# Unit-matrix products that nothing reads, put ahead of some forty waits of TensorE in a two-stage transformer kernel

## What is computed

```python
def first_block(x, c, ctx, c_ctx, w_mod, ...):          # two layers, streams x and z = ctx, 256 x 1024 each
    for l in range(DEPTH):
        mx = jnp.split((jax.nn.silu(c) @ w_mod[l] + b_mod[l])[:, None, :], N_MOD, axis=-1)
        mz = jnp.split(jax.nn.silu(c_ctx) @ w_mod[l] + b_mod[l], N_MOD, axis=-1)
        x = x + 0.5 * mx[2] * swiglu(modulate(rms_norm(x), mx[0], mx[1]), ffn1_w1[l], ffn1_w3[l], ffn1_w2[l])
        z = z + 0.5 * mz[2] * swiglu(modulate(rms_norm(z), mz[0], mz[1]), ffn1_w1[l], ffn1_w3[l], ffn1_w2[l])
        hx = modulate(rms_norm(x), mx[3], mx[4]) @ w_in[l]
        hz = modulate(rms_norm(z), mz[3], mz[4]) @ w_in[l]
        mix_x, mix_z = token_mixing(hx, hz, ...)         # Fourier, neighborhood, gated linear, grouped-query heads
        x = x + mx[5] * (mix_x @ w_out[l])
        x = x + 0.5 * mx[8] * swiglu(modulate(rms_norm(x), mx[6], mx[7]), ffn2_w1[l], ffn2_w3[l], ffn2_w2[l])
        if not last:                                     # the same two lines for z
...
def second_block(x, mem, positions, w_in, b_gate, ...):
    for l in range(DEPTH):
        h = x @ w_in[l]
        c_q, c_kv, k_pe, dq, dk, dv, mq, gate_pre = jnp.split(h, splits, axis=-1)
        o_mla = _mla_branch(...)                         # latent attention, 8 heads
        o_diff = _diff_branch(...)                       # differential attention, 8 heads x 2 maps
        o_mem = _mem_branch(mq, mem, mem_w_kv[l])        # attention to 256 rows of memory
        g = jax.nn.sigmoid(gate_pre.reshape(b, s, N_BRANCH, d) + b_gate[l])
        merged = g[:, :, 0] * (o_mla @ ...) + g[:, :, 1] * (o_diff @ ...) + g[:, :, 2] * (o_mem @ ...)
        x = _layernorm(DEEPNORM_ALPHA * x + merged @ w_out[l], ln1_g[l], ln1_b[l])
        f = jnp.square(jax.nn.relu(x @ mlp_w1[l])) @ mlp_w2[l]
        x = _layernorm(DEEPNORM_ALPHA * x + f, ln2_g[l], ln2_b[l])
    return x
```

## Time and profile before

| | |
|---|---|
| three runs | 3268.85, 3278.03, 3303.54 us; median 3278.03 |
| profiled execution | 3283.36 us; span from the first to the last instruction 3281.5 us |
| mean granted TensorE clock | 0.963 |
| busy: PE, DVE, ACT, POOL | 3116.6, 1765.1, 1506.8, 146.6 us |
| transfers | 552 MB read from memory, 169 GB/s |

### The profile page before, as it was taken

The page is one execution under the profiler, slowest core; times in us unless marked ns, Lnnn a source line. Parts: engine busy times, 40 slices in busy tenths (PEclk is TensorE's granted clock), DMA queues, the critical chain, the costliest instruction groups (busy, mean ns, idle before and its releaser), DMA issues.

```text
span 3281.5 us, 53932 instructions
## 1 busy us (share of the span) xinstructions
PE 3116.6 (95%) x22930; PEld 2821.6 (86%) x22930; DVE 1765.1 (54%) x2769; ACT 1506.8 (46%) x2294; POOL 146.6 (4%) x143
## 2 busy tenths in 40 slices
PE   7999999998999999999999899999998999999898
PEld 5899788897779998899898778999898898989887
DVE  3446544554436545446555434555666557576655
ACT  3345445453444443345444334446654444665443
POOL 0000100000000000000100000000110101101000
PEclk9999989998999999999999779999999999999999
DMA  7765435653535555765355335555345564434553
GB/s 260 263 206 168 155 117 169 229 185 116 155 121 191 179 181 191 253 218 169 129 171 169 103 105 191 180 168 155 121 150 186 168 204 151 142 113 153 178 191 131
DMA packets 465132, 556.66 MB, mean 170 GB/s; under 512 B 25421, under 2 KB 431869, under 8 KB 464509
## 3 DMA queue, kind: packets, MB, share of 16 engines
q1 hardware_dynamic: 464892, 553.21, 52.5%
HBM read 552.12 MB, written 1.05 MB: 169 GB/s over the span
## 4 chain that ended last, share of the span: by engine, by line
PE 81%; DVE 9%; DMA 3%; ACT 3%; issue 2%; SPq 1%; POOL 0%; DVEq 0%; ACTq 0%
PE psum L121 23%; PE psum L123 22%; PE psum L122 22%; DVE wl L2137 2%; DMA wr<-in_ffn_w_dram 2%; DVE wl L272 1%; PE psum L692 1%; PE psum L1492 1%; PE psum L2292 1%; PE psum L2398 1%; PE psum L2376 1%; PE psum L1848 1%; PE psum L1941 1%; PE psum L1479 1%; PE psum L1167 1%
## 5 line engine op out<-in xcount | busy, mean ns | idle before, releaser
L272 DVE TENSOR_TENSOR wl<-wr,wh 128x1024 fp32r<-128x1024 f32 (+1 forms) x558 | 656.8, 1212 | 241.8 <-ACT wh L261 240.5
L261 ACT ACTIVATE wh<-wr 128x1024 fp32r<-128x1024 f32 (+1 forms) x558 | 555.6, 1039 | 173.2 <-DMA wr<-in_ffn_w_dram 154.1
L121 PE MATMUL psum<-xt_hi,wh 128*128 128x256 f32 (+1 forms) x2000 | 574.2, 287 | 7.8 <-DVE wl L2137 4.8
L122 PE MATMUL psum<-xt_lo,wh 128*128 128x256 f32 (+1 forms) x2000 | 563.3, 282 | 0.0
L123 PE MATMUL psum<-xt_hi,wl 128*128 128x256 f32 (+1 forms) x2000 | 563.3, 282 | 0.0
L2137 DVE TENSOR_TENSOR wl<-wr,wh 128x1024 fp32r<-128x1024 f32 (+3 forms) x336 | 389.7, 1200 | 78.9 <-ACT wh L2129 77.6
L121 PEld LDWEIGHTS psum<-xt_hi,wh 128*128 128x128 f32 (+1 forms) x2000 | 380.1, 190 | 20.5 <-DVE wl L2137 8.3
L122 PEld LDWEIGHTS psum<-xt_lo,wh 128*128 128x128 f32 (+1 forms) x2000 | 379.7, 190 | 2.0
L123 PEld LDWEIGHTS psum<-xt_hi,wl 128*128 128x128 f32 (+1 forms) x2000 | 380.3, 190 | 0.1
L121 PE MATMUL psum<-wh,xt_hi 128*128 128x256 f32 (+1 forms) x1280 | 369.2, 288 | 4.3 <-DVE wl L272 2.4
L2129 ACT ACTIVATE wh<-wr 128x1024 fp32r<-128x1024 f32 (+3 forms) x336 | 322.6, 997 | 104.2 <-DMA wr<-in_mlp_w_dram 75.3
(11 more groups left out here) (489 smaller groups left out, 5505.4 us busy)
## 6 DMA issues: line engine op xcount, KB each, us to landing
wr<-in_ffn_w_dram SPq DMA_DIRECT2D x231, 1024.0 KB, 5.3
wr<-in_w_in_dram SPq DMA_DIRECT2D x88, 1024.0 KB, 5.2
wr<-in_w_mod_dram SPq DMA_DIRECT2D x72, 1024.0 KB, 5.1
wr<-in_mlp_w_dram SPq DMA_DIRECT2D x64, 1024.0 KB, 5.2
wr<-in_w_out_dram SPq DMA_DIRECT2D x20, 1024.0 KB, 5.0
wr<-in_mem_w_kv_dram SPq DMA_DIRECT2D x8, 1024.0 KB, 5.1
wr<-in_w_branch_dram SPq DMA_DIRECT2D x16, 512.0 KB, 3.5
wr<-in_w_branch_dram SPq DMA_DIRECT2D x8, 1024.0 KB, 5.0
```

The lines of the kernel that those rows point to most:

```text
L121: pe.matmul(out, a[0], b[0], start=first, stop=False)
L122: pe.matmul(out, a[0], b[1], start=False, stop=False)
L261: act.activation(self.high[s][:, r], self.raw[s][:, r], ACT.Copy).then_inc(self.highs.sem, 1)
L272: dve.tensor_tensor(self.low[s][:, r], self.raw[s][:, r], self.high[s][:, r].bitcast(F32), ALU.subtract).then_inc(self.lows.sem, 1)
```

## The change

Products `eye x eye` (128x128x128, float32, start and stop set) are issued by TensorE at chosen places, just ahead of one of its waits. Nothing reads their results. `stream` issues n of them. `Woven.cover` picks the bank: if the current unit has been claimed and nothing has been written to it yet (`untouched`), its bank; else the bank of the next unit, once that is free (a wait on `bank_free`, as `claim` has it). The first product of the piece sets start again, so what lay in the bank does not count. `touch` marks the bank as written. Pieces have a number `cover` (products ahead of the wait for their weights) and modulation pieces `cover_turn` (ahead of their first turn); stages of the first block have a table from step to number, applied by `Line.covered` before the generator of TensorE is advanced to that step. In the second block, the covers write to a bank that the stage uses next. In `UpPiece` the claim moves ahead of the wait for the weights. Besides single places, all 11 steps of `xm1.na` and of `xm1.gqa` get one product each.

```diff
--- before.py
+++ after.py
@@ -123,6 +123,12 @@
+def stream(pe, out, eye, n):
+
+    for _ in range(n):
+        pe.matmul(out, eye, eye, start=True, stop=True)
+
+
 def chunk_of(w2d, r0, nk, c0, cw):
@@ -210,7 +216,7 @@
         self.held = {4: [], 5: []}
-        self.follow = None
+        self.follow, self.next_unit, self.untouched = None, 0, False
@@ -312,8 +318,21 @@
             pe.wait_ge(self.bank_free[u % 2].sem, u // 2)
+        self.next_unit, self.untouched = u, True
         return self.ps[:, 6 + u % 2, :]
+    def touch(self):
+
+        if self.untouched:
+            self.next_unit, self.untouched = self.next_unit + 1, False
+
+    def cover(self, pe, n):
+
+        u = self.next_unit
+        if n and u >= 2 and not self.untouched:
+            pe.wait_ge(self.bank_free[u % 2].sem, u // 2)
+        stream(pe, self.ps[:, 6 + u % 2, 0:P], self.eye, n)
+
     def emptied(self, eng, u):
@@ -328,7 +347,7 @@
-    n_units, steps, fetch, parted = 1, 4, (), True
+    n_units, steps, fetch, parted, cover, cover_turn = 1, 4, (), True, 0, 0
@@ -393,7 +412,7 @@
     def __init__(self, w):
-        self.w, self.emitted = w, set()
+        self.w, self.emitted, self.cover = w, set(), {}
@@ -433,7 +452,7 @@
             if self.kind == "pe":
-                steps = s.pe(self.eng)
+                steps = self.covered(s)
             elif self.kind == "act":
@@ -445,6 +464,17 @@
             assert n == s.n_steps, (type(s).__name__, self.kind, n, s.n_steps)
+
+    def covered(self, s):
+
+        n, steps = 0, s.pe(self.eng)
+        while True:
+            s.w.cover(self.eng, s.cover.pop(n, 0))
+            got = next(steps, "over")
+            if got == "over":
+                return
+            n += got is None
+            yield got
@@ -553,6 +583,7 @@
         w, proj = self.w, self.proj
+        w.cover(pe, self.cover)
         wv = w.split(pe, self.m)
@@ -563,6 +594,7 @@
                     beat()
+                    w.touch()
                     cut = [proj.cut(v, k, i) for v in wv]
@@ -695,8 +731,10 @@
             u = self.u0 + 1 + i
+            w.cover(pe, self.cover_turn if i == 0 else 0)
             w.emptied(pe, self.mod.pieces[q].u0)
             w.claim(pe, u)
+            w.touch()
             for f in range(2):
@@ -781,12 +819,14 @@
         w, f_ = self.w, self.ffn
+        w.claim(pe, self.u0)
+        w.cover(pe, self.cover)
         wv = w.split(pe, self.m)
-        w.claim(pe, self.u0)
         beat = Beat(step, 16, self.steps)
...
                 beat()
+                w.touch()
                 if self.kind == 1 and self.i == 0 and f == 0 and k % 2 == 0:
@@ -2150,6 +2192,8 @@
+    cover = 0
+
     def __init__(self, w, chunks, lhs, emptied_by, empty, steps=2, turned=False, cut=None, need=None):
@@ -2182,6 +2226,10 @@
         for n, m in enumerate(self.ids):
+            if n == 0 and self.cover:
+                u = self.unit(0, 0)
+                pe.wait_ge(w.bank_free[u % 2].sem, u // 2)
+                stream(pe, w.ps[:, 6 + u % 2, 0:P], w.eye, self.cover)
             wv = w.split(pe, m)
@@ -2262,6 +2310,8 @@
+    cover = (0, 0, 0, 0)
+
     def __init__(self, w, src, width, nk, dst, need, room=None, split=True, gaps=(), scale=None):
@@ -2283,6 +2333,8 @@
                 yield
+            if b < len(self.cover):
+                stream(pe, self.w.ps[:, self.bank(b), 0:P], self.w.eye, self.cover[b])
             self.need(pe, b)
@@ -2780,6 +2832,7 @@
         self.w, self.b, self.ready, self.gain, self.shift, self.idle, self.room = w, b, ready, gain, shift, idle, room
+        self.cover = 0
         self.stats, self.centered_dve, self.centered_act = w.share("ln_stats", 1), w.share("ln_centered0", 1), w.share("ln_centered1", 1)
@@ -2793,6 +2846,7 @@
             yield
+        stream(pe, self.w.ps[:, 4, 0:P], self.w.eye, self.cover)
         pe.wait_ge(self.centered_dve.sem, self.centered_dve.at(1))
@@ -3355,6 +3409,7 @@
         m_t = Turn(w, lambda t, k: gate[k // 2][:, t, (k % 2) * P:(k % 2 + 1) * P], P, KT, mt, merged_in, gaps=[8, 5, 5, 5])
+        m_t.cover = (0, 0, 0, 9)
         segments.append(Segment([branches], [m_t]))
@@ -3371,6 +3426,7 @@
         outp.before_loads = out_loads
+        outp.cover, ln1.cover = 6, (11, 24)[l]
         pools.append(ln1)
@@ -3399,6 +3455,7 @@
             segments.append(Segment([mem_v], [ln2]))
+            ln2.cover = 10
             xt_ready = ln2.wait_done
@@ -3988,6 +4045,20 @@
     w.queue(order)
+    for p_, n in ((zf1.up1[0], 5), (zf1.down[4], 4), (xf2.up1[2], 4), (x_out1.pieces[0], 5), (zk.gate, 10), (xf3.up1[0], 2), (M1[35], 3)):
+        p_.cover = n
+    for p_, n in ((M1[13], 4), (M1[15], 3), (M1[25], 3), (M1[35], 5)):
+        p_.cover_turn = n
+    z_t0.cover = {1: 4}
+    x_t7.cover, z_t9.cover = {1: 2}, {1: 3}
+    zm.fourier.cover, xm1.fourier.cover = {2: 9}, {2: 7}
+    xm.decay.cover, xm1.decay.cover, zk.decay.cover = {0: 10}, {0: 7}, {0: 3}
+    zm.levels.cover, xm.levels.cover, xm1.levels.cover = {0: 1, 4: 2, 14: 6}, {0: 4, 8: 4}, {0: 3}
+    zm.st.cover, zk.state.cover, xm1.out.cover = {2: 8}, {0: 3}, {0: 3}
+    zm.na.cover, zm.gqa.cover = {8: 7}, {11: 7}
+    xm.bias_turn.cover, xm.na.cover, xm.gqa.cover = {0: 9}, {8: 3, 20: 4}, {11: 3, 23: 3}
+    zk.na_turn.cover, zk.g_turn.cover = {0: 18}, {0: 9}
+    xm1.na.cover, xm1.gqa.cover = {n: 1 for n in range(xm1.na.n_steps)}, {n: 1 for n in range(xm1.gqa.n_steps)}
```

## The result

The changed kernel takes 3238.35 us (median of 4 runs, 3232.32 to 3239.45) against 3277.83 us (median of 4 runs of the kernel before): a ratio of 0.9867, 95% interval 0.9834 to 0.9901. So it is faster, by 1.3%: by 39.5 us between the medians, and by 45.7 us between the two profiled executions (3283.36 and 3237.68 us; spans 3281.5 and 3235.9). The forecast was 3220, with 3200 to 3235 as its own range and 3190 to 3264 as the whole; the measured time lies in the whole range, 3 us above the forecast's own. The mean granted clock went from 0.963 to 0.987.

The account below looks back on a forecast made before the run. TensorE, busy 95% of the span, loses 100 us to its low clock. 72.7 us given back, less a tenth, 4.8 and 1.5, leaves 59: 3224 us, less 5.3 for the median, said as 3220; range 3190 to 3264.

Parts of the forecast that it names:

- The unit products hold the clock: Unit products in TensorE's waits keep its clock high: low stretches shrink from 240.6 us to some 60 to 90.
- Rival 1: Unit products don't hold the clock: low stretches stay, products are paid; 3289 us, chance 0.07.
- The clock's term: Time the clock gives back over TensorE's low stretches, busy time x 0.47: 72.7 us together.
- Nothing from the new wait: Waiting for the next bank to be read out, ahead of the products: bounds 0 and 5.8 us, taken as 0.
- the sign that the prediction named against itself: Waits on bank releases showing ahead of the unit products would count as wrong; no size given.
- Price of one: One unit product on TensorE takes 0.22 us at the high level, 0.41 us at the low one.
- Rival 2: The last x attention stays low: 18.5 us less gained, 2 us more for products; 3241 us, chance 0.18.
- Which stretches go: Clock gain by stretch: long attention 20.6 us, four uncovered 0, four with open waits 7.2, other 23 44.9.
- Rival 3: The falls move: half of the 119 us stays, all of the 30, attention goes half the time; 3250 us, chance 0.21.
- Rival 4: Nearly all low time goes, the uncovered stretches too; 3190 us, chance 0.07.
- What hides them: Products ahead of waits cost nothing until the wait ends; 1.5 us taken for shrunken waits, 4.8 for the attention's 22.
- What is late next: Earlier products find VectorE and ScalarE less far: a tenth of the 72.7 us gain goes to longer waits, leaving 65.4.

Follow-up runs that it names:

- waits_only: Changed kernel with its waits for banks and the earlier claim kept but no unit product issued: 3278.2 us, ratio 1.0010 to the kernel before.
- topped: trimmed plus more products where the changed kernel still idled behind them: 3235.95 us, ratio 0.9885 to the kernel before.
- attention_only: Changed kernel with only the 22 products of the last x attention kept, the other 265 left out: 3278.88 us, ratio 1.0020 to the kernel before.
- the repeat: The changed kernel run once more, nothing altered: 3235.25 us, ratio 0.9849 to the kernel before.
- trimmed: Changed kernel with 25 products fewer, where its trace showed them running past the wait's end: 3241.09 us, ratio 0.9890 to the kernel before.
- double: Changed kernel with twice the products in each of the 44 places, attention unchanged: 3270.79 us, ratio 0.9985 to the kernel before.
- na_steps_only: Changed kernel without the products in the second half (groups) of the last x attention: 3252.22 us, ratio 0.9927 to the kernel before.
- no_attention: Changed kernel without the 22 products of the last x attention, the other 265 kept: 3253.2 us, ratio 0.9915 to the kernel before.

## Why the prediction was right, point by point

**The unit products hold the clock: right.** Low time went to 81.8 us, in the foreseen 60 to 90; it goes back up to 133.5 us with half the products and stays at 218 us with the waits alone. Rival 1 is out. The clock's term was 72.7 us; measured are 68.7 in the same terms, and 69.9 from record to record.

**Nothing from the new wait: right for the wait, wrong for what stands behind it.** waits_only has 1.0010. But the step looked at the wait alone. The products stand behind it, so where the bank comes free late they come too late to fill anything: that is the sign that the prediction named against itself, and the trace has it at eleven places, with 4.9 us paid. Nor was there no wait of this kind in the trace before: the 3.42 us at 1977.2 are one.

**Price of one: right where no wait is near.** 0.20 us at full clock in the attention, against 0.22. For this part I had 20.6 x 0.9 - 4.8 = 13.7 us; both windows together went from 71.15 to 59.02 us, 12.1. The 22 steps with a product grew by 5.1 us, against 4.8. Rival 2 is out for the second half, but "I take it in full" was luck in part: the first half has a low course of 44 to 46 us even with its products, in topped and attention_only.

**Which stretches go: right in the sum, by two errors that cancel in part.** Three of the four uncovered are there (2389 isn't in the first profile, but in the repeat's), with 9.9 us of busy time in place of 19.6: 4.5 us given back by the price of the prediction, where I took 0. Of the four with a wait left open, 51.1 and 1976.2 are shorter, 750.8 and 948.8 as they were: 24.8 us of 30.4 stay, so 2.6 us came back and not 7.2. At all four the products stand behind a wait for a bank (1.96 us at 51.1, 1.06 at 750.8, 1.63 at 948.8, 3.33 at 1976.2), so they filled less of the wait than I had counted. All the rest, the long stretch and the other 23, went from 163.4 us to 32.6: 61.5 us against 65.5. Rival 3, whose range begins at 3238, wanted half of the 119 us of the other 23 to stay, and that is not so in this profile; but that the falls move from run to run is true, as the repeat shows. Rival 4 wanted the uncovered to go too, and they didn't.

**What hides them: the step that was mis-sized.** "I find no place where the products at 0.22 us are longer than the wait" compared each group with the bracket in the profile, and took 1.5 us. Measured are 11.0 us at the 44 places. The bracket is the whole idle time, and the products stand behind the first of its waits: the weights at 354 (2.2 us), the new wait for a bank at eleven places (4.9 us). At three places (2.6 us) the reading was wrong even of the trace before: four products ahead of nothing, and five ahead of instructions that waited for nothing, with more products ahead of the one short wait behind them.

**What is late next: right.** I left 7.3 us to waits that grow; all the other idle places grew by 8.0, the chunk at 1273 among them. That makes the sum: 72.7 - 1.5 - 4.8 - 7.3 = 59.1 foreseen, 69.9 - 11.0 - 5.1 - 8.0 = 45.8 measured, and of the 13.3 between them 9.5 are the products. trimmed, meant to show them, has 4 us less of them in its trace and no gain in its time; double shows that products past the end of the wait are paid for the most part.

**The number.** 3220 was 18 us low. The gain between profiled executions, 45.7 us against 59, is 13 of them; the other 5 are the offset that I subtracted, as the profiled run of before lay above its median and that of after doesn't. The repeat's profile gained 58.8 us, so 59 is within what an execution of this kernel can do, though by other terms: 82 us of clock and 23 paid.

## What to carry to other kernels

If TensorE falls to 1.2 GHz behind waits of one to three microseconds, the time lost is not the wait but the dense work behind it at half speed; sum the busy time of the low windows before deciding on anything (and look whether the record behind a window starts later than in a profile without it: a low stretch of 27 us, with the DMA engines busy all through, cost nothing here), and fill the waits to most of their length, but not beyond: double the number gave the gain back. Take the length of a wait not from the last bracket alone: look where the filler would stand in the queue, since a second semaphore ahead of it makes it exposed. The filler needs a place to write, and if that is a bank that has yet to be freed, it stands behind one more wait. In a part of small products that is near the edge, a product a step is worth its 0.2 us: 11 of them bought 13 us.

## What the runs showed of the hardware

The same instructions have two lasting courses. The second half of the attention ran dense at 0.50 for 34 us in na_steps_only and at 1.00 from start to end with one product of 0.2 us more in each step of 2.5 to 2.8 us; the first half did the one and the other with the same products in it. The runs of no_attention lie in two groups too (about 3250 and 3269 us), with no change in the program; the one profile is of the upper, with both halves low, and that the lower group has one half high is likely but not shown.

Transposes of the unit matrix held the clock as well as products (0.990 and 0.987 to 0.988).

Five of the profiles, the changed kernel's repeat among them, have a low stretch of 27 us from 15 to 43 us after the start, in the same products of the modulation that run at full clock in the other profiles. It costs no time there (the record behind it starts at 47.9 us in the repeat and in the kernel before).
